# Moving fillers, a value tile, two weight splits and one sum in the order of a two-block kernel

## The reference

```python
def first_block(x, ...):
    h = _rms(x, norm_mix_g[l])
    x = x + _mixer(h, ...)            # z = h @ w_in + b_in, three mixers, y @ w_out
    h = _rms(x, norm_ffn_g[l])
    x = x + _conv_glu(h, w_up[l], ffn_conv_w[l], ffn_conv_b[l], w_down[l])

def _mixer(h, ...):
    oa = _fox_attention(qa, ka, _heads(a_v, A_HEADS), ca)      # 8 heads of 64
    ob = _mlstm_chunkwise(...)                                 # 4 heads
    oc = _hgrn2_chunkwise(...)                                 # 4 heads, chunks of 16
    y = jnp.concatenate([ya, yb, yc], axis=-1)
    return y @ w_out

def second_block(x, ...):
    o_diff = causal_multimap_attention(dq, dk, dv, weights, ...)   # 4 heads, two maps each
    cq = rms_norm(cq, mla_q_norm[layer])
    q = (cq @ w_uq[layer])        # nope part: 4 heads of 128
    o_mla = causal_multimap_attention(mq, mk, mv, ...)             # 4 heads
    merged = sigmoid(g_diff) * (o_diff @ w_proj_diff) + sigmoid(g_mla) * (o_mla @ w_proj_mla)
    x = x + merged @ w_out[layer]
```

## Time and profile before

| | us |
|---|---|
| median of 3 runs | 1079.6 (1079.48 to 1079.92) |
| profiled execution | 1079.3 |
| its span, first to last instruction | 1077.5 |
| PE busy | 1062.5 |
| DVE busy | 743.0 |
| ACT busy | 449.8 |
| mean granted clock of TensorE | 0.998 |

### The profile page before, as it was taken

The page is one execution under the profiler, slowest core; times in us unless marked ns, Lnnn a source line. Parts: engine busy times, 40 slices in busy tenths (PEclk is TensorE's granted clock), DMA queues, the critical chain, the costliest instruction groups (busy, mean ns, idle before and its releaser), DMA issues.

```text
span 1077.5 us, 13675 instructions
## 1 busy us (share of the span) xinstructions
PE 1062.5 (99%) x5375; PEld 846.7 (79%) x5377; DVE 743.0 (69%) x1199; ACT 449.8 (42%) x704; POOL 2.8 (0%) x6
## 2 busy tenths in 40 slices
PE   9999999999999999999999999999999999999997
PEld 6777877866878888888888888887776776888886
DVE  6998877868678887854588745655568536464498
ACT  6512656367542223222222234654357543242264
POOL 0000000000000000000000000000000000000000
PEclk9999999999999999999999999999999999999999
DMA  8422122131213323233422135333120322033223
GB/s 282 126 79 79 42 76 77 42 119 40 80 62 105 117 79 107 59 89 115 139 79 87 51 98 156 79 117 118 44 79 3 116 78 79 1 118 117 82 74 99
DMA packets 100639, 96.64 MB, mean 90 GB/s; under 512 B 5968, under 2 KB 91232, under 8 KB 100576
## 3 DMA queue, kind: packets, MB, share of 16 engines
q1 hardware_dynamic: 99856, 94.71, 27.9%
q0 software_dynamic: 544, 1.05, 0.6%
q10 hardware_dynamic: 176, 0.02, 0.0%
HBM read 93.65 MB, written 2.10 MB: 89 GB/s over the span
## 4 chain that ended last, share of the span: by engine, by line
PE 90%; DVE 5%; ACT 3%; issue 2%; DVEq 0%; ACTq 0%
PE ring L1154 23%; PE ring L1156 23%; PE ring L1155 23%; PE bank L1154 3%; PE bank L1156 3%; PE bank L1155 3%; PE bank L1620 1%; DVE w_lo L2117 1%; PE bank L1318 1%; PE bank L1644 1%; PE bank L1593 1%; PE bank L1250 1%; PE bank L1385 1%; PE bank L1357 1%; DVE bank L2110 1%
## 5 line engine op out<-in xcount | busy, mean ns | idle before, releaser
L1154 PE MATMUL ring<-act_hi,w_hi 128*128 128x512 f32 (+2 forms) x808 | 320.5, 397 | 0.5 <-DVE xT L2492 0.5
L1156 PE MATMUL ring<-act_hi,w_lo 128*128 128x512 f32 (+2 forms) x808 | 313.9, 388 | 0.0
L1155 PE MATMUL ring<-act_lo,w_hi 128*128 128x512 f32 (+2 forms) x808 | 313.6, 388 | 0.0
L1726 ACT ACTIVATE w_hi<-w_raw 128x2048 fp32r<-128x2048 f32 (+5 forms) x95 | 157.9, 1663 | 251.7 <-PE ring L1156 201.0
L2117 DVE TENSOR_TENSOR w_lo<-w_raw,w_hi 128x2048 fp32r<-128x2048 f32 (+4 forms) x100 | 188.0, 1882 | 4.0 <-ACT w_hi L1726 3.8
L1154 PEld LDWEIGHTS ring<-act_hi,w_hi 128*128 128x128 f32 x808 | 151.9, 188 | 36.5 <-issue 3.9
L1155 PEld LDWEIGHTS ring<-act_lo,w_hi 128*128 128x128 f32 x808 | 152.0, 188 | 31.3 <-issue 1.9
L1156 PEld LDWEIGHTS ring<-act_hi,w_lo 128*128 128x128 f32 x808 | 151.8, 188 | 31.4
L1155 PE MATMUL ring<-hidL,w_hi 128*128 128x512 f32 x176 | 68.6, 390 | 0.0
L1154 PE MATMUL ring<-hidH,w_hi 128*128 128x512 f32 x176 | 68.5, 389 | 0.0
L1156 PE MATMUL ring<-hidH,w_lo 128*128 128x512 f32 x176 | 68.5, 389 | 0.0
(11 more groups left out here) (420 smaller groups left out, 1663.1 us busy)
## 6 DMA issues: line engine op xcount, KB each, us to landing
w_raw<-in_w_in SPq DMA_DIRECT2D x30, 1024.0 KB, 5.3
w_raw<-in_w_up SPq DMA_DIRECT2D x22, 1024.0 KB, 5.1
w_raw<-in_w_out SPq DMA_DIRECT2D x6, 1024.0 KB, 5.3
w_raw<-in_w_down SPq DMA_DIRECT2D x8, 768.0 KB, 4.7
w_raw<-in_w_down SPq DMA_DIRECT2D x8, 640.0 KB, 4.3
w_raw<-in_w_in SPq DMA_DIRECT2D x7, 512.0 KB, 4.8
xin<-in_xt SPq DMA_DIRECT2D x8, 256.0 KB, 4.2
xT<-in_xt SPq DMA_DIRECT2D x2, 1024.0 KB, 6.7
```

The costliest lines, as they stand in the source:

```text
L1154: pe.matmul(out, ah, bh, start=(first and n == 0), stop=False)
L1155: pe.matmul(out, ah, bl, start=False, stop=False)
L1156: mm = pe.matmul(out, al, bh, start=False, stop=(last and n == len(pairs) - 1))
L1726: return act.activation(out, src, func, **more)
```

## The change

No operation is added or taken away except that one weight split is made in two halves. Five places of the order change:

1. In the HGRN2 section the `w_lo` of chunk 4 (first chunk of `b_qk`) is no longer placed whole behind the gates tile but in two halves, one before and one behind the next `hg_att` product.
2. In fox, the value tile `a_v` 1 stands whole in unit 1 and no longer half in unit 1, half in unit 2.
3. In fox, `wo_b` 0 to 4 are spread anew, one or two k steps at a time, over units 5 to 24, and the split of the first `wo_a` chunk moves: its `w_hi` from unit 17 to 21, its `w_lo` halves from units 18 and 20 to 22 and 23.
4. Before the second norm the square and sum of `wo_a` 6 stand behind tile 7.
5. In dif, `qn` 0 is spread over units 12 to 14 (one k step each) and finished in 14, no longer made in 15, and `qn` 1 moves from unit 17 to 15. A helper `query` does part of such a tile.

```diff
--- before.py
+++ after.py
@@ -496,9 +496,14 @@
             stage("cb_a", b)
             if b == 0:
                 tile(("gates", 0))
+                stage("hold_lo", True)
                 stage("gates", 0)
                 stage("gate_ln")
+                stage("lo", 2)
             fill_slot()
+            if b == 0:
+                stage("lo", 2)
+                stage("hold_lo", False)
         for b in range(NB):
             in_tile("cb", b, "cb1")
             stage("hold_lo", b < NB - 1)
@@ -655,12 +660,12 @@
 
         WO_A = chunk_of["wo_a0"]
         attention("fox", AH, "ya", {
-            0: [("ml_o", 3)], 1: [("yb_norm",), ("a_v", 2, "a_v1"), ("a_v", 1, 1)], 2: [("a_v", 1, "a_v0"), ("yb", 0), ("y_split", 2)],
+            0: [("ml_o", 3)], 1: [("yb_norm",), ("a_v", 2, "a_v1"), ("a_v", 1, "a_v0")], 2: [("yb", 0), ("y_split", 2)],
             3: [("y_low", 2), ("yb", 1), ("a_v", 3, 1)], 4: [("y_split", 3), ("y_low", 3), ("a_v", 3, "a_v1"), ("hold_lo", True)],
-            5: [("wo_b", 0, 2)], 6: [("wo_b", 0, 4)],
-            7: wo_b(0), 8: [("wo_b", 1, 2)], 10: [("wo_b", 1, 4)], 11: wo_b(1), 12: [("wo_b", 2, 2)],
-            14: [("wo_b", 2, 4)], 15: wo_b(2),
-            16: [("wo_b", 3, 2)], 17: [("w_later", WO_A)], 18: [("wo_b", 3, 4), ("lo", 2)], 19: wo_b(3), 20: [("lo", 2)], 22: [("wo_b", 4, 2)], 24: [("wo_b", 4, 4)], 25: wo_b(4),
+            5: [("wo_b", 0, 2)], 7: [("wo_b", 0, 3)], 8: [("wo_b", 0, 4), ("wo_b", 1, 2)], 9: wo_b(0), 10: [("wo_b", 1, 4)], 11: wo_b(1),
+            12: [("wo_b", 2, 1)], 14: [("wo_b", 2, 2)], 16: [("wo_b", 2, 4)], 17: wo_b(2) + [("wo_b", 3, 1)], 18: [("wo_b", 3, 3)],
+            20: [("wo_b", 3, 4)], 21: wo_b(3) + [("w_later", WO_A)], 22: [("lo", 2)], 23: [("wo_b", 4, 1), ("lo", 2)],
+            24: [("wo_b", 4, 4)], 25: wo_b(4),
             29: [("wo_b", 5, 2)], 31: [("wo_b", 5, 4)], 32: [("w_later", WO_A + 1)], 33: [("lo", 2)] + wo_b(5), 34: [("wo_b", 6, 2), ("lo", 2)], 35: [("wo_b", 6, 4)],
             36: wo_b(6) + [("wo_b", 7, 2), ("wo_b", 7, 4)], 37: wo_b(7), 39: [("hold_lo", False)]})
 
@@ -672,7 +677,10 @@
                 stage("wo_a", j)
             else:
                 in_tile("wo_a", j, f"wo_a{j // 4}")
-            stage("n_sq", 0, j)
+            if j == KD - 1:
+                stage("n_sq", 0, j - 1)
+            if j != KD - 2:
+                stage("n_sq", 0, j)
             if j < KD // 2:
                 stage("n_split", 0, j)
         stage("n_last", 0)
@@ -789,9 +797,12 @@
         fill[7].insert(0, ("gate_act", "dg"))
         assert next(gates, None) is None
         fill[10].append(("hold_lo", True))
-        fill[15].append(rest_of("qn", 0))
+        for k in range(2):
+            fill[12 + k].append(("qn", 0, k + 1))
+        fill[14].append(rest_of("qn", 0))
+        fill[15].append(rest_of("qn", 1))
         fill.update({
-            16: [rest_of("qr", 0), ("lo",)], 17: [rest_of("qr", 1), ("qr_rot", 0), ("qr_rot", 1), rest_of("qn", 1)], 18: [rest_of("qn", 2)],
+            16: [rest_of("qr", 0), ("lo",)], 17: [rest_of("qr", 1), ("qr_rot", 0), ("qr_rot", 1)], 18: [rest_of("qn", 2)],
             19: [rest_of("qn", 3), rest_of("kn", 0), rest_of("kn", 1)],
             20: [rest_of("kn", 2), ("lo",), rest_of("kn", 3)], 22: [rest_of("mv", 0), rest_of("mv", 1), ("lo",), ("hold_lo", False)]})
         attention("dif", 4, "yd", fill)
@@ -1185,6 +1196,15 @@
                     pairs = [((ah[:, k, b * P:b * P + P], al[:, k, b * P:b * P + P]), (wh[:, k, :], wl[:, k, :])) for k in range(KD)]
                     mm = product(out[:, 256 * s:256 * s + 256], pairs)
                 if until == 2:
+                    mm.then_inc(tile_done, 1)
+
+            def query(name, begun=0, until=3):
+
+                out = at_ring(name) if begun else open_bank(name)
+                wh, wl = weights("uqn", name[1])
+                mm = product(out[:], [((wh[:, k, :], wl[:, k, :]), (latH[k][:], latL[k][:])) for k in range(begun, until)],
+                             first=(begun == 0), last=(until == 3))
+                if until == 3:
                     mm.then_inc(tile_done, 1)
 
             def keep_warm(n, out):
@@ -1454,6 +1474,10 @@
                     channels(s[1:3], "cq1", 0, act, part=1, begun=s[3], until=s[4])
                 elif kind == "begin" and s[1] == "lat":
                     channels(s[1:3], LAT_OF[s[2]], (0, P, 0, 0, P)[s[2]], act, begun=s[3], until=s[4])
+                elif kind == "begin" and s[1] == "qn":
+                    if s[2:4] == (0, 0):
+                        pe.wait_ge(lat_lo, 3)
+                    query(s[1:3], s[3], s[4])
                 elif kind == "begin" and s[1] == "gate":
                     def first(k):
                         pe.wait_ge(n_lo, k + 1)
@@ -1551,15 +1575,14 @@
                     out = open_bank(s)
                     pe.wait_ge(lat_sum, 2 + i)
                     pe.matmul(out[:], cc("ones"), latS[(2, 3)[i]][:], start=True, stop=True).then_inc(tile_done, 1)
-                elif kind in ("qn", "qr", "kn"):
+                elif kind == "qn":
+                    query(s, begun.get(s, 0))
+                elif kind in ("qr", "kn"):
                     i = s[1]
                     if i == 0:
                         pe.wait_ge(lat_lo, 5 if kind == "kn" else 3)
                     out = open_bank(s)
-                    if kind == "qn":
-                        wh, wl = weights("uqn", i)
-                        st = [(wh[:, k, :], wl[:, k, :]) for k in range(3)]
-                    elif kind == "qr":
+                    if kind == "qr":
                         wh, wl = weights("uqr")
                         st = [(wh[:, k, P * i:P * i + P], wl[:, k, P * i:P * i + P]) for k in range(3)]
                     else:
```

## The result

The changed kernel takes 1083.62 us (median of 6 runs, 1082.95 to 1086.68) against 1079.69 (6 runs, 1079.48 to 1079.92): ratio 1.004, 95% interval 1.0029 to 1.005. It is slower by 3.9 us, where I had said 1.8, with a range up to 1083.6. The runs also lie further apart than before: 3.7 us against 0.4. One run of a later experiment (1514.27 us, mean clock 0.654) fell in a state in which TensorE is held at a much lower clock, and is left out of its comparison.

The account below looks back on a forecast made before the run. TensorE, busy 1062.5 of 1077.5 us, was taken as the bound. Terms of -0.85, +0.05, +2.05, 0 and +0.6 summed to +1.85 on the profiled 1079.3, giving a median forecast of 1081.4 us, range 1076.4 to 1083.6.

Parts of the forecast that it names:

- Part 1: HGRN2 section: halving the w_lo split starts Ab 1.08 us earlier and removes TensorE's wait, -0.85 us.
- the restart beside the wait of 0.79: HGRN2, before line 1250: small restart expected to go together with TensorE's 0.79 us wait for Ab, -0.85 in all.
- Part 2: Fox start: a_v 1 whole in unit 1 shrinks the yb wait, but a_v 3 loses it again, +0.05 us.
- Part 3: Fox: new fillers gain, but the moved split's halves lengthen the chain to unit 26's scores, +2.05 us.
- Part 4: Before the second norm: the later square of wo_a 6 has over 1 us before its result is needed, 0.
- Part 5: Dif: the qn drain delays PT by 0.6 us; 2.1 us freed become a wait before kn, +0.6 us.
- Slower by the clock: Rival: TensorE's clock falls in part 3's near 3 us gap, costing 1.9 us more, 1083.3 us; chance 0.12.
- my +1.85: Whole kernel: the five edits' terms -0.85, +0.05, +2.05, 0 and +0.6 us added up.

Follow-up runs that it names:

- the second occasion: The unaltered changed kernel run again, on the same chip as the two kernels with a single gap filled: median 1084.56 us, 4.7 us above the kernel before.
- the 3.9 us gap: Kernel before with only the wo_a split moved (w_hi to unit 21, halves to 22 and 23), fillers as before: 1085.36 us (1.0055).
- the kernels with products in the fox gap: Changed kernel with 13 constant products before unit 26's scores: with dif's qn edit undone, 1081.83 us; with 10 more before kn 0, 1083.39 us.
- The kernel with both gaps filled: Changed kernel plus unused products on constants, 13 before unit 26's fox scores and 10 before kn 0: 1083.39 us (1.0031).
- the split where it was: Changed kernel with the first wo_a chunk's split back in units 17, 18 and 20, fillers in their new places: 1079.62 us (0.9994).
- part 5 alone: Kernel before with only the new places of the qn steps in dif: 1081.84 us (1.0015).
- the kernel with products ahead of kn 0: Changed kernel plus 10 unused products on constants before kn 0 in dif: 1083.30 us (1.0034).

## Why the prediction was wrong

- **Part 1** was right in mechanism and small in size: -0.85 said, -1.04 in the trace, beyond its bound of -0.9. The term I had mis-sized is the restart beside the wait of 0.79: the 16 products took 2.59 us with the wait in them (43.39 to 45.98), and take 1.58 in one row.
- **Part 2**: +0.05 said, 0.0 to 0.01. The wait moved from `yb` to `a_v` 3, as worked out.
- **Part 3**: +2.05 said, +2.29. The experiments bear out the pieces: fillers -1.2 with the split left in its old place, second half 1.05. From the gap of 3.25 with both halves, 2.1 with one and 1.0 with none, each is 1.1 us. The 0.15 by which the exponentials of unit 22 were to start earlier didn't come. The scores of unit 24 waited 0.66, not 0.9, and those of unit 18 0.59, not 0.
- **Part 4**: 0, as said.
- **Part 5**: +0.6 said, +0.61 (0.48 at the values of unit 13, 0.13 more at kn 0). The `PT` copy and the wait of 2.35 us ahead of kn 0 came as forecast (about 2.5).
- **The step that failed** is the one after the sum, "Slower by the clock": a chance of 0.12, for the fox gap alone. The waits add up to +2.0, within 0.2 of my +1.85. The other 1.9 of the median (2.7 on the second occasion) is the clock, which falls in one gap or in both: of the two profiles one has the fall in dif alone, the other both. I had worked out two gaps, 3 and 2.5 us, both about twice as long as the longest of before (1.29), and gave the fall of the clock to the one only. A single fall costs 1.2 to 1.6 in these traces and 2.7 behind the 3.9 us gap; I had said 1.9. That this case's 1083.3 lies 0.3 from the median measured is thus partly luck: it has one fall at too high a price, where the runs have one or two.

I had let the absence of falls behind waits up to 1.29 us speak against one behind longer waits, on which it is silent. The rule of the Trainium skill that I set beside it (TensorE: Matmul & The Clock Gate, Part 1: The HAM clock gate), that an idle TensorE goes back to the throttled clock, was the better guide, and this case's trace agrees, with a granted clock of 0.72 in the stretch behind 2.35 us of idle time.

What stays open: why the load before the second block's norm lands 0.6 us later in the kernels with products in the fox gap, and so how much of the median the fox gap's clock alone makes up (0.9 by the medians, each against its own before, and about 1.5 if that load is left out). The kernel with both gaps filled stands at +3.4, so the +2.0 of the waits alone has been added up from traces and never measured as a time.

## What to carry to other kernels

In a kernel whose TensorE never rests, an idle gap has two prices: its length, and behind a gap of 2 us or more here, in half to most of the runs, 1.2 to 2.7 us more at half the clock. So a weight split belongs where no engine's chain is waited for, and filling many small waits by emptying one later place can make one long gap of it, which is worse than the waits were. A single profile may miss this: the spread of the runs showed the fall at the fox gap before a trace did. The mean clocks help less, since they also count the low clock at the start of the program: 0.998 stands in runs of either group.

## What the runs showed of the hardware

- The same gap, 2.35 us ahead of kn 0, had the clock fall in three profiled executions (the changed kernel's two and the split where it was; 0.63 us a product) and not in a fourth, part 5 alone (0.39). Of four profiles with a gap of 3.2 to 3.3 us ahead of unit 26 two show a fall behind it and two don't. So the length alone does not decide it in one execution. No profiled execution showed one behind a gap of up to 1.3 us.
- The fall need not come with the gap. In the changed kernel the first two products behind it (845.87 and 846.18) still run at 2.4 GHz, those from 846.45 on at 1.2, and from 849.82 on at 2.4 again; in its second profile all of kn 0 still runs at 2.4. In the kernel with products ahead of kn 0 the scores behind the fox gap are slow from the first (2.08 us where 1.13 is usual).
